# A convolution layer norm with its variance about a pivot, and the convolution stage's instructions in another order

## The reference

```python
a, b = jnp.split(rmsnorm(x, norm_g) @ pw1_w + pw1_b, 2, axis=-1)
h = a * jax.nn.sigmoid(b)
h = depthwise_causal_conv(h, dw_w) + dw_b          # 31 taps for each channel
mu  = jnp.mean(h, axis=-1, keepdims=True)          # over the 1024 channels
var = jnp.mean(jnp.square(h - mu), axis=-1, keepdims=True)
h = (h - mu) * lax.rsqrt(var + 1e-6) * ln_g + ln_b
return jax.nn.silu(h) @ pw2_w + pw2_b
```

## Time and profile before

| | |
|---|---|
| median of 3 runs | 1121.08 us (1120.88 to 1122.82) |
| the profiled execution | 1122.06 us |
| its span | 1120.3 us |
| TensorE busy | 1059.0 us, 95% |
| VectorE busy | 663.5 us, 59% |
| ScalarE busy | 500.8 us, 45% |
| mean granted TensorE clock | 0.98 |

### The profile page before, as it was taken

One profiled execution on the slowest core, in us unless ns is written; L12 is line 12 of the kernel. 1 busy time (PEld: TensorE's weight loads), 2 busy tenths in 40 slices (PEclk: granted clock), 3 DMA queues, 4 the chain that ended last, 5 costly groups with the idle time before them and its releaser, 6 DMA issues.

```text
span 1120.3 us, 17101 instructions
## 1 busy us (share of the span) xinstructions
PE 1059.0 (95%) x7243; PEld 935.4 (83%) x7243; DVE 663.5 (59%) x1014; ACT 500.8 (45%) x709; POOL 65.8 (6%) x109
## 2 busy tenths in 40 slices
PE   6986899999999978999999999999999999999997
PEld 6963698999989945899999989988667989999996
DVE  4956456555566598555655567847445546555554
ACT  5313344444444456445444445535344545343432
POOL 2000066000000000000000001000000000000000
PEclk9997899999999989999999999999899999999999
DMA  8865237665553700657566555644124515656540
GB/s 230 219 180 150 74 115 217 182 198 172 184 146 100 240 1 1 209 148 223 173 183 199 171 180 170 190 159 162 66 75 151 189 38 188 206 171 204 172 151 38
DMA packets 188998, 174.28 MB, mean 156 GB/s; under 512 B 12822, under 2 KB 164502, under 8 KB 188922
## 3 DMA queue, kind: packets, MB, share of 16 engines
q1 hardware_dynamic: 187216, 169.67, 49.9%
q10 hardware_dynamic: 1322, 2.62, 0.7%
q0 software_dynamic: 384, 0.90, 0.2%
HBM read 171.24 MB, written 1.93 MB: 155 GB/s over the span
## 4 chain that ended last, share of the span: by engine, by line
PE 81%; DVE 10%; ACT 3%; DMA 3%; issue 2%; ACTq 0%; SPq 0%; POOLq 0%; POOL 0%; DVEq 0%
PE bank L1709 24%; PE bank L1710 24%; PE bank L1711 24%; DVE split_lo L1030 2%; PE bank L1891 2%; ACT split_hi L639 1%; DVE xn_lo L1047 1%; DVE soft L1317 1%; DMA pt<-in_cmp_pos_v 1%; PE bank L1746 1%; DMA act<-u_rows 1%; DVE soft L1336 1%; DMA raw<-in_a_pw_w 1%; PE bank L2171 1%; PE bank L2172 1%
## 5 line engine op out<-in xcount | busy, mean ns | idle before, releaser
L1030 DVE TENSOR_TENSOR split_lo<-raw,split_hi 128x2048 fp32r<-128x2048 f32 (+1 forms) x157 | 356.6, 2277 | 185.8 <-ACT split_hi L639 185.5
L1709 PE MATMUL bank<-xn_hi,split_hi 128*128 128x256 f32 x1456 | 415.4, 285 | 5.8 <-DVE xn_lo L1047 5.2
L1710 PE MATMUL bank<-xn_lo,split_hi 128*128 128x256 f32 x1456 | 411.8, 283 | 0.0
L1711 PE MATMUL bank<-xn_hi,split_lo 128*128 128x256 f32 x1456 | 411.7, 283 | 0.0
L639 ACT ACTIVATE split_hi<-raw 128x2048 fp32r<-128x2048 f32 (+1 forms) x157 | 296.6, 1893 | 130.3 <-PE bank L1711 123.8
L1709 PEld LDWEIGHTS bank<-xn_hi,split_hi 128*128 128x128 f32 x1456 | 278.0, 191 | 12.1 <-issue 4.4
L1710 PEld LDWEIGHTS bank<-xn_lo,split_hi 128*128 128x128 f32 x1456 | 278.1, 191 | 1.5
L1711 PEld LDWEIGHTS bank<-xn_hi,split_lo 128*128 128x128 f32 x1456 | 278.1, 191 | 0.0
L1709 PE MATMUL bank<-split_hi,ffa_hi 128*128 128x512 f32 x320 | 125.4, 392 | 1.8 <-DVE ffa_lo L1030 1.8
L1710 PE MATMUL bank<-split_lo,ffa_hi 128*128 128x512 f32 x320 | 124.9, 390 | 0.0
L1711 PE MATMUL bank<-split_hi,ffa_lo 128*128 128x512 f32 x320 | 124.5, 389 | 0.0
(11 more groups left out here) (289 smaller groups left out, 944.9 us busy)
## 6 DMA issues: line engine op xcount, KB each, us to landing
raw<-in_ffn_w_in SPq DMA_DIRECT2D x88, 512.0 KB, 5.2
raw<-in_w_ff SPq DMA_DIRECT2D x32, 1024.0 KB, 5.4
raw<-in_ffn_w_out SPq DMA_DIRECT2D x22, 1024.0 KB, 4.9
raw<-in_w_in SPq DMA_DIRECT2D x14, 1024.0 KB, 5.3
raw<-in_a_pw_w SPq DMA_DIRECT2D x16, 512.0 KB, 7.3
raw<-in_w_xkv SPq DMA_DIRECT2D x8, 1024.0 KB, 5.6
raw<-in_a_pw_w SPq DMA_DIRECT2D x4, 1024.0 KB, 8.7
raw<-in_b_w_in SPq DMA_DIRECT2D x4, 1024.0 KB, 5.9
```

Source lines behind the costliest of these rows:

```text
L1030: return nc.vector.tensor_tensor(dst, src, hi.bitcast(F32), ALU.subtract)
L1709: mm(dst, left[0], right[0], start=start, stop=False)
L1710: mm(dst, left[0], right[1], start=False, stop=False)
L1711: return mm(dst, left[1], right[0], start=False, stop=stop)
```

## The change

The variance is taken about a pivot, p, in place of about the mean. The pivot is the channel mean of tiles 2, 3 and 4, estimated as 8/3 times their sum under `mean_w`. With m the mean, var = mean((h-p)^2) - (m-p)^2, bounded below by zero. The squares of h-p can be computed before m is known; they lie in `u`, whose tiles are free by then. `mean` is 3/8 of p plus the sum of the other five tiles, `offset` is m-p. The sum of squares is taken on VectorE for tiles 0 to 5 (into two tiles), and four products add those two, tile 6 and tile 7.

- TensorE: one conv behind each of the projections of tiles 4, 5 and 6; the sums of the three pivot tiles directly behind tile 7's projection, and ahead of convs 3 to 5; a second bank for the sums of the other tiles.
- ScalarE: the emptying of convs 0 to 2 before the sigmoids of tiles 5 to 7, convs 3 and 4 right behind the last sigmoid, and only then the split and, behind the first square, the small transfers. A one-column root and a one-column SiLU stand ahead of the real ones.
- VectorE: gatings before taps 1, 4, 8, 13, 19 and 26 (`glu_at`) in place of every fourth; the pivot and the first subtraction before tap 28; the centring of `v` becomes four instructions of two tiles each, two of them between the SiLU halves; pw2's third piece is split at the end.

In the diff, lines are moved eight columns to the left and blank lines are left out.

```diff
+pivot, offset, mean, ln_rstd = [softf[:, S * n:S * n + S] for n in range(4, 8)]
...
+PIVOT = CONV_PE[0:3]
+SQUARES = [slice(2, 5), slice(5, 7), slice(0, 2), slice(7, 8)]
...
-halved = sem("halved")
+pivot_ready = sem("pivot_ready")
+var_ready = sem("var_ready")
...
+    def conv_evac(n):
+        ft = CONV_PE[n]
+        sc.wait_ge(quad_done, n + 1)
+        nc.scalar.activation(v[:, ft, :], bank[4 + n % 4][:, 0:S], ACT.Identity,
+                             bias=vecT[:, col["a_dw_b"] + ft:col["a_dw_b"] + ft + 1]
+                             ).then_inc(conv_out, 1)
+    def square_about_pivot(j):
+        sc.wait_ge(centred, j + 1)
+        part = u[:, SQUARES[j], PAD:PAD + S]
+        nc.scalar.activation(part, part, ACT.Square).then_inc(squared, 1)
...
+        if ft >= 5:
+            conv_evac(ft - 5)
...
+    conv_evac(3)
+    conv_evac(4)
...
+    square_about_pivot(0)
...
-    for n, ft in enumerate(CONV_PE):
-        sc.wait_ge(quad_done, n + 1)
-        nc.scalar.activation(v[:, ft, :], bank[4 + n % 4][:, 0:S], ACT.Identity,
-                             bias=vecT[:, col["a_dw_b"] + ft:col["a_dw_b"] + ft + 1]
-                             ).then_inc(conv_out, 1)
-    for j in range(2):
-        sc.wait_ge(centred, j + 1)
-        nc.scalar.activation(actf[:, D * j:D * j + D], vf[:, D * j:D * j + D],
-                             ACT.Square).then_inc(squared, 1)
-    sc.wait_ge(stat_done, 2)
-    nc.scalar.activation(softf[:, 0:S], bank[1][:, 0:S], ACT.Sqrt, bias=eps_col[:, :]).then_inc(std_ready, 1)
+    square_about_pivot(1)
+    conv_evac(5)
+    square_about_pivot(2)
+    square_about_pivot(3)
+    nc.scalar.activation(msq[:, 18:19], eps_col[:, :], ACT.Sqrt)
+    sc.wait_ge(var_ready, 1)
+    nc.scalar.activation(ln_rstd, ln_rstd, ACT.Sqrt, bias=eps_col[:, :]).then_inc(std_ready, 1)
+    nc.scalar.activation(msq[:, 17:18], eps_col[:, :], ACT.Silu)
...
-    tasks = []
-    for ft in range(2, KT):
-        tasks.append(lambda ft=ft: glu_pw1(ft))
-        if ft - 2 < len(CONV_PE):
-            tasks.append(lambda n=ft - 2: quad_weights(n))
-    tasks += [lambda j=j: through(chunk_of["pw2"][j]) for j in range(3)]
+    def about_pivot(j):
+        part = u[:, SQUARES[j], PAD:PAD + S]
+        for n, ft in enumerate(CONV_PE):
+            if ft in range(KT)[SQUARES[j]]:
+                ve.wait_ge(conv_out, n + 1)
+                ve.wait_ge(u_stored[n], 16)
+        nc.vector.tensor_tensor(part, v[:, SQUARES[j], :], pivot.unsqueeze(1).broadcast_to(
+            [P, len(range(KT)[SQUARES[j]]), S]), ALU.subtract).then_inc(centred, 1)
+    glu_at = {1: 2, 4: 3, 8: 4, 13: 5, 19: 6, 26: 7}
...
-        if j % 4 == 1:
-            for task in tasks[:2]:
-                task()
-            tasks = tasks[2:]
+        if j in glu_at:
+            glu_pw1(glu_at[j])
+            quad_weights(glu_at[j] - 2)
+        if j == 28:
+            ve.wait_ge(stat_done, 1)
+            nc.vector.tensor_scalar(pivot, bank[0][:, 0:S], KT / len(PIVOT), None,
+                                    ALU.mult).then_inc(pivot_ready, 1)
+            ve.wait_ge(pivot_ready, 1)
+            about_pivot(0)
...
-    for task in tasks:
-        task()
+    about_pivot(1)
+    ve.wait_ge(conv_dve, 2)
+    about_pivot(2)
+    ve.wait_ge(squared, 2)
+    link(nc.vector.tensor_tensor(u[:, 2:4, PAD:PAD + S], u[:, 2:4, PAD:PAD + S], u[:, 4:6, PAD:PAD + S], ALU.add))
+    ve.wait_ge(squared, 3)
+    nc.vector.tensor_tensor(u[:, 0:2, PAD:PAD + S], u[:, 0:2, PAD:PAD + S], u[:, 2:4, PAD:PAD + S],
+                            ALU.add).then_inc(squares_summed, 1)
+    about_pivot(3)
...
+    def centre(g):
...
-    ve.wait_ge(stat_done, 1)
-    for j in range(2):
-        part = v[:, 4 * j:4 * j + 4, :]
-        nc.vector.tensor_tensor(part, part, bank[0][:, 0:S].unsqueeze(1).broadcast_to([P, 4, S]),
-                                ALU.subtract).then_inc(centred, 1)
-    for j in range(2):
-        ve.wait_ge(squared, j + 1)
-        x = nc.vector.tensor_tensor(actf[:, D * j:D * j + 512], actf[:, D * j:D * j + 512],
-                                    actf[:, D * j + 512:D * j + D], ALU.add)
-        if j == 0:
-            x.then_inc(halved, 1)
-    ve.wait_ge(halved, 1)
-    link(x)
-    link(nc.vector.tensor_tensor(actf[:, 0:512], actf[:, 0:512], actf[:, D:D + 512], ALU.add))
-    nc.vector.tensor_tensor(actf[:, 0:S], actf[:, 0:S], actf[:, S:2 * S], ALU.add).then_inc(squares_summed, 1)
+        part = v[:, 2 * g:2 * g + 2, :]
+        link(nc.vector.tensor_tensor(part, part, mean.unsqueeze(1).broadcast_to([P, 2, S]),
+                                     ALU.subtract))
+    ve.wait_ge(stat_done, 2)
+    share = len(PIVOT) / KT
+    link(nc.vector.scalar_tensor_tensor(out=offset, in0=pivot, scalar=share - 1.0, in1=bank[2][:, 0:S],
+                                        op0=ALU.mult, op1=ALU.add))
+    nc.vector.scalar_tensor_tensor(out=mean, in0=pivot, scalar=share, in1=bank[2][:, 0:S],
+                                   op0=ALU.mult, op1=ALU.add)
+    link(nc.vector.tensor_tensor(offset, offset, offset, ALU.mult))
+    centre(0)
+    ve.wait_ge(stat_done, 3)
+    link(nc.vector.tensor_tensor(ln_rstd, bank[1][:, 0:S], offset, ALU.subtract))
+    nc.vector.tensor_scalar(ln_rstd, ln_rstd, 0.0, None, ALU.max).then_inc(var_ready, 1)
+    centre(1)
...
-    link(nc.vector.reciprocal(softf[:, S:2 * S], softf[:, 0:S]))
+    link(nc.vector.reciprocal(ln_rstd, ln_rstd))
...
-        nc.vector.tensor_tensor(part, part, softf[:, S:2 * S].unsqueeze(1).broadcast_to([P, 2, S]),
+        nc.vector.tensor_tensor(part, part, ln_rstd.unsqueeze(1).broadcast_to([P, 2, S]),
...
+            centre(g + 2)
...
+    through(chunk_of["pw2"][2])
...
-        for n in {4: [0], 5: [1, 2], 6: [3]}.get(ft, []):
-            conv(n)
+        if 4 <= ft < 7:
+            conv(ft - 4)
...
-        x = mm(bank[0][:, 0:S], mean_w[:, :], v[:, ft, :], start=ft == order[0], stop=ft == order[-1])
-        if ft == order[-1]:
+        x = mm(bank[0 if ft in PIVOT else 2][:, 0:S], mean_w[:, :], v[:, ft, :],
+               start=ft in (order[0], order[len(PIVOT)]),
+               stop=ft in (PIVOT[-1], order[-1]))
+        if ft in (PIVOT[-1], order[-1]):
...
+    def square_sum(ft, n):
+        te.wait_ge(squared, n)
+        return mm(bank[1][:, 0:S], mean_w[:, :], u[:, ft, PAD:PAD + S], start=ft == 0, stop=ft == 7)
...
-    te.wait_ge(glu_done, 5)
-    for n in (4, 5):
-        conv(n)
-        for m in range(4) if n == 4 else [4]:
-            channel_sum(CONV_PE[m])
-    for ft in CONV_DVE + CONV_PE[-1:]:
+    te.wait_ge(glu_done, KT)
+    for ft in PIVOT:
+        channel_sum(ft)
+    conv(3)
+    conv(4)
+    channel_sum(CONV_PE[3])
+    channel_sum(CONV_PE[4])
+    conv(5)
+    for ft in CONV_DVE:
...
-    te.wait_ge(glu_done, KT)
...
-    mm(bank[1][:, 0:S], mean_w[:, :], actf[:, 0:S], start=True, stop=True).then_inc(stat_done, 1)
+    for ft in (0, 1, 6):
+        square_sum(ft, 3)
+    channel_sum(CONV_PE[5])
+    square_sum(7, 4).then_inc(stat_done, 1)
```

## The result

| | before | changed |
|---|---|---|
| median of the runs beside each other | 1121.95 us (4 runs, 1120.88 to 1124.09) | 1111.32 us (4 runs, 1109.8 to 1113.68) |
| ratio | | 0.9908, 95% interval 0.9879 to 0.9937 |
| the profiled execution, its span | 1122.06, 1120.3 us | 1110.95, 1109.2 us |

The change is 10.6 us faster by the medians (7 to 14 us by the interval of the ratio), 11.1 by the two profiled executions. Forecast was 1108.5, a gain of 12.6; the measured time lies in the range.

The account below looks back on a forecast made before the run. TensorE, busy for 95% of the span, was taken as the bound, so only its waits and slow clock could be won: 5.6 us from term 1, the rest from emptyings and statistics, 12.6 in all, giving 1108.5 us; range 1105.5 to 1115.

Parts of the forecast that it names:

- Term 1: Tile 6's projection runs before conv 2 and covers its wait for copies: 5.57 us net, 4.09 wait and 1.48 slow clock.
- The rival that tile 6's projection waits at 60.8: Tile 6's projection waits for something that also ended at 64.9: gain only 7.0 us, 1114.1; chance 0.07.
- VectorE's cover: Between the gatings of tiles 6 and 7, table, 14 taps and a split end at 76.7, gating ready at 76.8.
- Term 2: Conv banks emptied early, so only gating 7 holds TensorE; conv 5 ends at 90.6, 10.7 us earlier than before.
- Term 3: Statistics about the pivot, between conv 5 and pw2: 12.2 us in place of 14.1, pw2's first product at 102.8.
- The bounds: Transfer landings before convs 4 and 5 and a warmer clock could shift the likely gain to 8.3 to 15.5 us.
- the late copies: Tile 6's store and the next copies each land after 8.6 us; conv 4 idles 4.8: gain 4.9, 1116.2; chance 0.13.
- Slower, by a cold TensorE: TensorE stays at 1.2 GHz from tile 7's projection to the statistics: 7.8 us slower, 1128.9; chance 0.03.
- The table load: ScalarE's load for SiLU, 1.28 us, runs under the reciprocal and costs nothing; with a 1.38 us drain the gain is 12.3.
- Behind pw2: Two added centrings and the later split of pw2's third piece cost nothing, margins 7 and 17 us; later work moves forward.

Follow-up runs that it names:

- before again: The kernel before, unchanged, run and profiled once more for a second trace: 1120.39 us.
- two taps more: The changed kernel with the last gating at tap 28 in place of 26: 1113.48 us, ratio 0.992.
- 29 products: The changed kernel plus 29 unread products before pw2: alone 1108.48 us; with SiLU halves of tiles 2 and 3 ahead of the last two centrings 1111.33 us.
- 24 products: The changed kernel plus 24 products of mean_w by itself, which nobody reads, before pw2: 1112.11 us, ratio 0.9895.

## Why the prediction was right, point by point

- **Term 1** (tile 6's projection before conv 2, 5.6 us): the sigmoid of tile 7 was forecast at 76.32 and came at 76.71, in a run that reached tile 5's store 0.39 later: exact. Its size was exact only against the one trace it was read from. The trace of before again has 1.58 us of stop and no slow conv in its place. This is the term that was mis-sized, and the chance that the draw was a large one stands nowhere in the prediction: "Net 5.57: the wait of 4.09 and 1.48 of slow clock" took one landing of one transfer for the kernel's. In the other trace of before the same term is worth about 1.7 (24.32 less 22.67), and 4.09 is the longest such stop that any of the fourteen traces has or would have had. The rival that tile 6's projection waits at 60.8 is out: TensorE was busy for all of the 15.20 us from 60.80 on.
- **VectorE's cover** ("the 14 taps just fit"): 0.17 us to spare, and shown by the kernel with two taps more. The stop ahead of the sums was forecast at 1.0 and is 1.13.
- **Term 2**: nothing but gating 7 holds TensorE, all convs warm, conv 5 ends at 91.30 against 90.6, 0.39 of it the start. What the prediction did not say is that this term can't stand alone: the emptying without conv 3 as a cover gains about 2 us, and on top of the order of convs 2 and 3 nothing that is resolved.
- **Term 3**: pw2 forecast at 102.8, measured 103.44, so 0.25 late when the start is taken off. The statistics about the pivot bring 1.51 us of it. The one-column activations bring nothing by the rows of before, where the loads lie ahead of the waits without them; no run of the pivot's statistics left them out.
- **The bounds and the late copies.** Tile 6's store was issued at 68.46 and held its copies until 75.83: 7.4 us, nearly the longest landing. But its copies then landed in 4.4, at 80.26, and conv 4 started at 82.74. As worked out, the cover sufficed: in all nine traces with the changed order of convs neither conv 4 nor conv 5 waited. Conv 5 has the smaller margin: tile 7's copies landed at 85.79 (86.0 forecast), 1.8 us ahead of it, and 1.7 to 2.3 in the nine.
- **Slower, by a cold TensorE**: out, the clock was 1.00 from 60.8 to 96 us. The Trainium skill (TensorE: Matmul & The Clock Gate, Part 1) says that activity releases the slow state; the trace agrees, over stops of 1.13 and 0.89 us.
- **The table load**: the root ends at 98.49, the load runs from 98.51 to 99.79, the one-column SiLU starts at 99.80, and the real one at 101.10, released by VectorE. The Trainium skill (ScalarE: Activation LUTs, What ACT_TABLE_LOAD costs) adds a drain of about 1.38 us to each switch of tables; the trace does not agree, there is no such pause on either side of the load. Nothing was lost.
- **Behind pw2**: the split of pw2's third piece ended at 111.6 and was not waited for. But "all later work is unchanged and moves forward" was 0.9 us too simple: 0.54 was given back because pw2's start stayed slow for 4.8 us in place of 3.6, and 0.43 in attention. Neither is shown to belong to the change. From pw2's first product to its second bias product took 4.45 to 5.42 us in the kernels with the old statistics and 4.76 to 5.42 in those with the pivot and no filler. Attention took 127.4 to 128.0 us in twelve traces, 125.4 and 129.5 in the two with 29 products; the granted clock in it was 0.96 in the profiles of before and after, 0.99 in the shortest and 0.95 in the longest. The difference of 0.43 at the same clock stays open.

The sum: 12.6 forecast, 12.39 measured from tile 5's store; less 0.39 of start, 0.54 at pw2's start and 0.43 in attention it is 11.0, and the profiled executions differ by 11.11. The mechanism was right, and the closeness of the figure is in part luck. The sum was read from a trace of before with the longest stop of all, and was held first against that same trace. By the other trace of before the same working gives 8.4 (12.6 less the 4.24 between 56.91 and 52.67, an estimate). The medians show 10.6, between the two, which fits a before whose stop varies as the fourteen landings do.

## What to carry to other kernels

A stop that ends on a transfer is a draw, not a length: take a second trace of the kernel before, lined up on an event ahead of the stop, before its size goes into a sum. When waits stand in a row, ask of each removal what the next instruction waits for and whether work is left to cover it; here emptying alone, or with half of the reorder, only moved the stop to conv 5, and one more conv between gating and copies made the difference. And an engine that must stand still before a dense stretch can bring a slow clock into it (here behind stops of 1.41 us and more, not behind each), so the last wait can cost more than its length. Last, look in the trace of before whether a trick is needed: both table loads already lay ahead of their waits.

## What the runs showed of the hardware that I had not expected

- After the same stop of 3.85 us, conv 4 took 6.50, 6.18 and 4.97 us in three traces: how long the slow level lasts differs from run to run for the same work. A conv 5 behind a stop of 3.03 took 6.52, one behind 2.83 took 5.35.
- After a stop of 1.41 us behind busy work pw2 began at the full level, fell to the slow one within its first products and stayed there for over 3 us, while it was busy all the time (24 products). After 0.30 us it stayed at 1.00. In before again and with the early emptying, conv 2 ran at a granted clock of 1.00 (3.66 us) behind stops of 1.58 and 1.79. So the length of the stop alone does not tell whether the clock falls.
- The copies of tile 4 were issued between 54.4 and 60.7 us in the fourteen traces and landed between 62.9 and 67.1. The time from the first issue to the landing went from 5.0 us (two taps more, issued at 60.71) to 10.8 (24 products, issued at 56.33). Late issue went with a short landing in most of them, but no run shows what sets it.
- A table load of ScalarE starts behind the instruction before it and not behind the wait of the activation that needs it (110.57 against 113.10 in before), so the load was hidden without any help.
